# Retention stage of a hybrid decoder step: transposes over two sets of PSUM banks, query products after them, ScalarE spreads the sample queries; a sigmoid and squares move into a weight stream

## What is computed

```
q, k, v, g_ret = jnp.split(ret_cols.astype(f32), 4, axis=-1)
q = rotary(q...) * (RET_DK ** -0.5);  k = rotary(k...)
# retention_chunked, per chunk of tokens and head:
scores = jnp.einsum('bihd,bjhd->bhij', qc, kc) * dmat
o = jnp.einsum('bhij,bjhv->bihv', scores, vc)
o = o + jnp.einsum('bihd,bhdv->bihv', qc, s) * q_dec[None, :, :, None]
s = s * s_dec[None, :, None, None] + jnp.einsum('bjhd,jh,bjhv->bhdv', kc, k_dec, vc)
out_a = jax.nn.silu(g_ret) * head_norm(o, RET_GN_EPS)
...
gates = jax.nn.sigmoid(gate_cols.reshape(bsz, t, N_BRANCH, D_MODEL))
merged = jnp.sum(gates * jnp.einsum('btnc,ncd->btnd', branches, p['w_branch'][l]), axis=2)
...
m = rmsnorm(mem, p['mem_norm'][l])      # needs the squares of mem
```

## Time and profile before

| | us |
|---|---|
| median of 3 runs (lowest, highest) | 3109.57 (3106.17, 3111.55) |
| profiled execution, its own time | 3115.79 |
| span of its profile | 3114.1 |
| mean granted TensorE clock, share of full | 0.958 |

### The profile page before, as it was taken

How to read it: one execution, slowest core, us unless ns; L and a number is a source line. 1 busy time by engine, 2 the same in 40 slices (tenths; PEclk the granted TensorE clock), 3 DMA queues, 4 the chain that set the end, 5 groups by cost and what they waited for, 6 DMA issues and landing times. The chain is left out here.

```text
span 3114.1 us, 63966 instructions
## 1 busy us (share of the span) xinstructions
PE 2844.1 (91%) x25694; PEld 2645.1 (85%) x25694; DVE 1755.5 (56%) x2645; ACT 1253.0 (40%) x1739; POOL 521.4 (17%) x341
## 2 busy tenths in 40 slices
PE   7998989989988999899999988989898899998997
PEld 7998888777787898799889978987787788887997
DVE  4444764586576565544354458445756766655443
ACT  4534522254323443444254355222542234434542
POOL 0003650054400000000000046401543000000000
PEclk9999999999998999899999999999999989998998
DMA  4444340135374466344344443401454554663443
GB/s 164 148 148 140 118 141 18 37 115 181 109 278 162 158 211 220 129 149 148 116 152 148 149 134 112 126 24 34 138 176 144 224 213 128 221 222 119 149 148 105
DMA packets 119694, 448.21 MB, mean 144 GB/s; under 512 B 13648, under 2 KB 23920, under 8 KB 111664
## 3 DMA queue, kind: packets, MB, share of 16 engines
q1 hardware_dynamic: 97920, 329.78, 32.9%
q0 software_dynamic: 21552, 115.34, 10.1%
HBM read 397.04 MB, written 48.02 MB: 143 GB/s over the span
## 5 line engine op out<-in xcount | busy, mean ns | idle before, releaser
L1532 ACT ACTIVATE w_high<-ring 128x1024 fp32r<-128x1024 f32 x598 | 631.8, 1057 | 761.1 <-PE gemm_banks L902 320.9
L898 PE MATMUL gemm_banks<-in_high,w_high 128*128 128x320 f32 (+1 forms) x2720 | 802.3, 311 | 26.9 <-ACT w_high L1532 14.7
L1936 DVE TENSOR_TENSOR w_low<-ring,w_high 128x1024 fp32r<-128x1024 f32 x436 | 532.7, 1222 | 477.4 <-ACT w_high L1532 476.7
L899 PE MATMUL gemm_banks<-in_low,w_high 128*128 128x320 f32 (+1 forms) x2720 | 794.7, 308 | 0.0
L733 POOL TENSOR_TENSOR w_low<-ring,w_high 128x1024 fp32r<-128x1024 f32 x162 | 414.0, 2564 | 968.1 <-ACT w_high L1532 966.6
L898 PEld LDWEIGHTS gemm_banks<-in_high,w_high 128*128 128x128 f32 x2720 | 514.3, 189 | 33.8 <-issue 14.7
L899 PEld LDWEIGHTS gemm_banks<-in_low,w_high 128*128 128x128 f32 x2720 | 514.1, 189 | 1.7
L902 PE MATMUL gemm_banks<-in_high,w_low 128*128 128x320 f32 (+1 forms) x2720 | 451.0, 308 | 6.9 <-POOL w_low L733 3.9
L902 PEld LDWEIGHTS gemm_banks<-in_high,w_low 128*128 128x128 f32 x2720 | 408.8, 189 | 9.9 <-POOL w_low L733 5.1
L947 PE MATMUL gemm_banks<-in_high,w_high 128*128 128x320 f32 x640 | 209.2, 339 | 21.8 <-DVE arena L2062 16.7
L974 PE MATMUL gemm_banks<-act_high,w_high 128*128 128x320 f32 x704 | 208.3, 309 | 2.6 <-DVE arena L1985 2.6
(11 more groups left out here) (414 smaller groups left out, 4229.4 us busy)
## 6 DMA issues: line engine op xcount, KB each, us to landing
ring<-in_w SPq DMA_DIRECT2D x598, 512.0 KB, 3.6
arena<-in_kc POOLq DMA_DIRECT2D x14, 1024.0 KB, 6.6
arena<-in_vc POOLq DMA_DIRECT2D x14, 1024.0 KB, 7.3
out_fill<-stage SPq DMA_DIRECT2D x80, 160.0 KB, 4.0
arena<-in_ssm POOLq DMA_DIRECT2D x16, 512.0 KB, 13.6
out_s_ssm<-arena POOLq DMA_DIRECT2D x16, 512.0 KB, 14.0
arena<-in_ret POOLq DMA_DIRECT2D x16, 512.0 KB, 22.2
out_s_ret<-arena POOLq DMA_DIRECT2D x16, 512.0 KB, 7.1
```

The costliest lines, as they stand in the source:

```text
L898: mm(dst, w_high[:, slot, w(k)], in_high[:, k, 0:n], start=(k == 0), stop=False)
L899: mm(dst, w_high[:, slot, w(k)], in_low[:, k, 0:n], start=False, stop=False)
L1532: f(w_high[:, slot], ring[:, s, 0:D], ACT.Copy).then_inc(weights_high, 1)
L1936: tt(w_low[:, slot], ring[:, pos % RING, 0:D], w_high[:, slot].bitcast(F32), ALU.subtract).then_inc(weights_split, 1)
```

## The change

TensorE's three blocks of transposes go to banks 4 to 7, 0 to 3 and 4 to 7; the second waits for no copies, the third for those of the first. VectorE makes `qd` after the second block's copies, the eight sample products as one with a repeated table, and zeroes both mask buffers with two large memsets right after the third block. ScalarE writes the eight samples' queries into them, in eight copies after its own part of the transposes. In `ssd_out`'s stream, gate(2) now stands ahead of the split of chunk 4 and the squares of `mem` ahead of that of chunk 6.

```diff
--- before.py
+++ after.py
@@ -306,14 +306,13 @@
 def ret_steps(engine):
 
     if engine == "A":
-        return ["silu"] + [("tr", tb) for tb in range(3)]
-    out = ["qd"] if engine == "V" else []
-    out += [("tr", tb) for tb in range(3)]
+        return ["silu"] + [("tr", tb) for tb in range(3)] + ["qm"]
+    out = []
+    out += [("tr", 0), ("tr", 1), "qd", ("tr", 2), "qz"] if engine == "V" else [("tr", tb) for tb in range(3)]
     steps = [(tb, q) for tb in range(3) for q in range(2)]
     for m in range(6):
         out += [(*steps[m], "score")]
         out += [(*steps[m - 1], "out")] if 0 < m < 5 else []
-        out += ["qm"] if m == 2 and engine == "V" else []
     out += [("only", 0), ("only", 1)] if engine == "V" else []
     out += [("read", 0), ("read", 1), (2, 0, "out"), (2, 1, "out")]
     for j in range(4):
@@ -1319,14 +1318,14 @@
                 pe.wait_ge(psum_free, evacuated["ret"])
                 arrived(pe, layer, "vg_back")
                 for tb, (c0, n) in enumerate(TBS):
-                    if tb:
-                        need(V, ("tr", tb - 1))
-                        need(A, ("tr", tb - 1))
+                    if tb == 2:
+                        need(V, ("tr", 0))
+                        need(A, ("tr", 0))
                     for k in range(16):
-                        ins_ = tr(bank(4 + k // 4)[0:n, (k % 4) * P:(k % 4 + 1) * P], qkvg[:, 8 + k, c0:c0 + n], K("ident"))
+                        ins_ = tr(bank((4, 0, 4)[tb] + k // 4)[0:n, (k % 4) * P:(k % 4 + 1) * P], qkvg[:, 8 + k, c0:c0 + n], K("ident"))
                     hit(ins_, M, ("tr", tb))
-                need(A, ("tr", 2))
-                need(V, ("tr", 2))
+                need(A, ("tr", 1))
+                need(V, ("tr", 1))
                 steps = [(tb, q) for tb in range(3) for q in range(2)]
 
                 def score(m):
@@ -1381,7 +1380,7 @@
                     if 0 < m < 5:
                         out(m - 1)
                 arrived(pe, layer, "ret_states_here")
-                need(V, "qm")
+                need(A, "qm")
                 read(0)
                 read(1)
                 out(4)
@@ -1822,8 +1821,14 @@
                 A_.mark(f(qkvg[:, 24:32], qkvg[:, 24:32], ACT.Silu), A, "silu")
                 for tb, (c0, n) in enumerate(TBS):
                     need(M, ("tr", tb))
-                    A_(f(vtk[0:n, tb, 0:512], bank(6)[0:n, 0:512], ACT.Copy))
-                    A_.mark(f(vtk[0:n, tb, 512:1024], bank(7)[0:n, 0:512], ACT.Copy), A, ("tr", tb))
+                    A_(f(vtk[0:n, tb, 0:512], bank((6, 2, 6)[tb])[0:n, 0:512], ACT.Copy))
+                    A_.mark(f(vtk[0:n, tb, 512:1024], bank((7, 3, 7)[tb])[0:n, 0:512], ACT.Copy), A, ("tr", tb))
+                need(V, "qz")
+                for j in range(4):
+                    qm = (qm01, qm23)[j // 2][:, j % 2].rearrange("p a (b t) -> p a b t", t=SL)
+                    for b in (j, 4 + j):
+                        ins_ = f(qm[:, :, b], qd[:, :, P + b * SL:P + (b + 1) * SL], ACT.Copy)
+                A_.mark(ins_, A, "qm")
                 ret_headnorm(hsq, hroot, K("eps")[:, 1:2])
 
             def gate(j):
@@ -1875,10 +1880,13 @@
                 high_parts("ssd", rb_back)
                 arrived(act_, layer, "gates_back")
                 gate(1)
-                stream("ssd_out")
-                gate(2)
-                arrived(act_, layer, "mem_here")
-                A_.mark(f(msq, mem, ACT.Square), n_sq, "mem")
+                def between(i, c):
+                    if c == 2:
+                        gate(2)
+                    if c == 4:
+                        arrived(act_, layer, "mem_here")
+                        A_.mark(f(msq, mem, ACT.Square), n_sq, "mem")
+                stream("ssd_out", between)
                 high_parts("rwkv", rc)
                 stream("rwkv_out")
                 act_.wait_ge(psum_free, evacuated["rwkv_out"])
@@ -2394,18 +2402,19 @@
             def retention():
                 V, A, M = rt["V"], rt["A"], rt["P"]
                 arrived(dve, layer, "rettab_here")
-                V_(tt(qd[:, :, 0:P], qkvg[:, 0:8, P:TP], qtab, ALU.mult))
-                for b in SAMPLES:
-                    ins_ = tt(qd[:, :, P + b * SL:P + (b + 1) * SL], qkvg[:, 0:8, TP + b * SL:TP + (b + 1) * SL],
-                              qtab[:, :, 0:SL], ALU.mult)
-                    V_(ins_) if b < NS - 1 else V_.mark(ins_, V, "qd")
                 for tb, (c0, n) in enumerate(TBS):
+                    if tb == 2:
+                        V_(tt(qd[:, :, 0:P], qkvg[:, 0:8, P:TP], qtab, ALU.mult))
+                        qs, qo = (v.rearrange("p a (b t) -> p a b t", t=SL) for v in (qkvg[:, 0:8, TP:T], qd[:, :, P:P + C64]))
+                        V_.mark(tt(qo, qs, qtab[:, :, 0:SL].unsqueeze(2).to_broadcast([P, 8, NS, SL]), ALU.mult), V, "qd")
                     need(M, ("tr", tb))
                     kd = K("kdec" if tb < 2 else "s_kdec", 0, n)
                     for g in range(2):
                         ins_ = tt(split(ktok[:, tb], 8, P)[0:n, 4 * g:4 * g + 4],
-                                  bank(4 + g)[0:n, :].rearrange("p (a b) -> p a b", b=P), each(kd[:, 4 * g:4 * g + 4], P), ALU.mult)
+                                  bank((4, 0, 4)[tb] + g)[0:n, :].rearrange("p (a b) -> p a b", b=P), each(kd[:, 4 * g:4 * g + 4], P), ALU.mult)
                         V_(ins_) if g == 0 else V_.mark(ins_, V, ("tr", tb))
+                V_(nc.vector.memset(qm23, 0.0))
+                V_.mark(nc.vector.memset(qtab, 0.0), V, "qz")
                 steps = [(tb, q) for tb in range(3) for q in range(2)]
 
                 def score(m):
@@ -2435,20 +2444,10 @@
                         V_(tt(Sp[:, hs], Sp[:, hs], each(K("sdec")[:, hs], P), ALU.mult))
                         V_.mark(tt(Sp[:, hs], Sp[:, hs], st, ALU.add), V, (tb, q, "out"))
 
-                def masked_queries():
-                    for j in range(4):
-                        qm = (qm01, qm23)[j // 2][:, j % 2].rearrange("p a (b t) -> p a b t", t=SL)
-                        V_(nc.vector.memset(qm, 0.0))
-                        for h in range(2):
-                            b = 4 * h + j
-                            ins_ = copy(qm[:, :, b], qd[:, :, P + b * SL:P + (b + 1) * SL])
-                            V_(ins_) if b < NS - 1 else V_.mark(ins_, V, "qm")
                 for m in range(6):
                     score(m)
                     if 0 < m < 5:
                         out(m - 1)
-                    if m == 2:
-                        masked_queries()
 
                 def only(j):
```

## The result

| | median us (lowest, highest), runs |
|---|---|
| before, same chips | 3114.18 (3106.17, 3128.78), 12 |
| changed | 3097.7 (3090.14, 3103.32), 12 |
| ratio, 95% interval | 0.9939 (0.9924, 0.9953) |

By the ratio the kernel became 19 us faster (14.6 to 23.7; the two medians differ by 16.5); 22.6 were forecast. The forecast's 3086.6 and its range up to 3096 stood against a before of 3109.57, from which 19 less is 3090.6; the before of these runs is 4.6 higher. The profiled execution took 3102.74 us, 5.0 above its median, with a span of 3101.2. So the spans differ by less (12.9) than the medians, and I read stages, not the whole.

The account below looks back on a forecast made before the run. TensorE was taken as the bound (matmuls fill 91% of the span), so its idle and low-clock time decide. Retention's 11 plus the stream's 11.6 make 22.6, taken as 23 off 3109.6: 3086.6 us, range 3079 to 3096.

Parts of the forecast that it names:

- Second stretch: From ssd_out to rwkv_out: idle 5.31 to 0.92 and first chunk at full clock, 5.8 us less a layer, 11.6 in all.
- table load: Sign of being wrong: a table load appearing around the sigmoid moved into ssd_out's stream; none stood there before.
- VectorE's low parts: Rival ahead of rwkv_out: these end the wait, so the stream move fails; only 11 us from retention, about 3099, chance 0.04.
- The low clock only moves: Sign of being wrong: the low clock leaves the changed places only to turn up in denser ones; no size given.
- Retention: Start of retention: 5.0 + 2.3 + 2 x 2.6 = 12.5 us less, taken as 11 after the clock.
- the memsets: Ahead of the first score step on VectorE: two of 128x1024, 0.91 us each, new there and hidden by nothing.
- The first score step on VectorE: In retention: 5.0 us earlier in the second layer, 2.3 in the first; second layer 10.5 us after the first transposes.
- The fourth product's wait: In retention: with the masks off VectorE, TensorE's 2.60 us gap closes, 2.6 less in each layer.
- the masks on ScalarE had their cover: Eight ScalarE copies, at most 2.7 us, end ten microseconds ahead of read, so they cost nothing.
- I take off 0.8 a layer, between nothing and 1.5: Retention's charge for low clock behind a new 3.6 us TensorE wait ahead of the first product.
- The rule on transposes: The skill says transposes do not count as busy for the clock gate; the prediction said the trace disagrees here.
- the low clock: Rival: low clock from the transposes on costs 3 to 5 us a layer; total 14 to 18, 3092 to 3096, chance 0.12.

Follow-up runs that it names:

- the changed kernel once more: The changed kernel run again unaltered, for a second profile and as the mark for others; ratio 0.9939 of before.
- four filled into the wait: Changed kernel with four added matmuls in TensorE's wait ahead of the first product with v and one ahead of out; ratio 0.9912 of before.
- before with five filled in: The kernel before with five added matmuls of constants in TensorE's 5.3 us wait ahead of rwkv_out; ratio 1.0003.
- banks only: The kernel before with transposes over two sets of banks and qd behind the second block's copies, masks still on VectorE; ratio 0.9954.
- the 64.16 of the table: Ssd_out to out, second layer, of the changed kernel with qd behind the second score step and both memsets on GpSimd; ratio 0.9882 of before.
- the whole wait filled (ten): The kernel before with ten added matmuls of constants in TensorE's wait ahead of rwkv_out's first chunk; ratio 1.0015.

## Why the prediction was right, and what it mis-sized

**Second stretch: right.** Forecast 5.8 us a layer; ssd_out to out lost 5.8 and 6.2. The idle went to 0.92, the chunk to 5.33, the splits kept their pace with 0.24 us left behind the sigmoid, no table load appeared, and VectorE's low parts did not end the wait.

**What was missing there.** "The low clock only moves" was named as a way to be wrong, not put into the sum. Out to memk took 16.1 us in nine of the twelve layers of kernels whose stream is unchanged, and about 17 in eight of ten layers where it is changed and the wait ahead of `out` is not filled. On the mean of these layers some 0.6 us of the 5.8 are given back.

**Retention: right in sum, by terms that were off in both directions.** Forecast 12.5 less 1.6 for the clock, 11 in all; the stage lost 5.0 and 5.6 in the profile, 4.8 a layer over the six layers of three profiles. The sum was luckier than its layers: with 0.8 off for the clock it has 4.1 for the first and 6.8 for the second. The first lost more because its first block met the full clock this time (1.94 us for the 3.18 of before) and because before had lost 1.6 behind its 2.6 wait there; the second lost less because of the memsets' waits and the clock. And a low clock in the first block, which `qd` used to hide, now costs: 1.66 us in two of the six layers, which the sum has for the first layer only. The first score step on VectorE came 11.05 us behind the first transposes against 10.56 worked out for full clock; the half microsecond is the 0.28 us that each memset waits. The fourth product's wait closed, as said, and the masks on ScalarE had their cover. The term that failed in size is the clock: "I take off 0.8 a layer, between nothing and 1.5". From the first product to the update the changed kernel takes 21.7 to 22.4 us, and 20.05 with the wait filled, so it costs 1.6 to 2.3, above my upper end. Against before it costs less: in three of the eight layers with the old retention TensorE fell to the low clock behind the wait of 2.6 (24.3 us from the first product to the update, 22.7 in the others), 0.6 on the mean, which leaves about 1.2 a layer for the change. The wait was 4.26 us, not 3.6, for the memsets' waits again.

**The step that the prediction did not take** was to price the two halves against each other. It credited 2.6 us to the masks' move and charged 1.8 for the memsets. The runs say: on top of the two sets of banks the move costs 1.4 to 2.0 us a layer up to the update (32.1 against the 33.5 to 34.2 of the four layers whose first block ran at full clock), since it puts 2.4 us ahead of the first score step and the low clock behind the longer wait, for a gap of 2.6. By itself it gains 1.3. So up to the update the gain is the banks' and `qd`'s, and the masks' part takes 1.4 to 2.0 of the seven microseconds away again. Up to ssd_out the difference is 0.8 on the mean, inside the spread, and the whole times (0.9954 and 0.9963, with overlapping intervals) do not tell the two apart.

**The rule on transposes.** The trace after agrees with the one before, against the rule that the prediction cites from the Trainium skill (TensorE: Matmul & The Clock Gate, Part 4: PE-mode transpose), whose figures there are for bf16 where these are fp32: 48 transposes in a row, and a granted clock at full (1.91 us a block, in the profile above) with the scores behind them. In five layers of the new orders the first block met the low clock, and the clock rose with nothing but transposes run, here in the first layer of the changed kernel once more:

```profile
913.90:917.00 3.10, 3.10 (x16) 3.10 (x15) 0.69 (x1) 2.10 (x1) 0.00 (x0) 0.50 0.25 100
917.30:919.50 2.20, 2.20 (x22) 2.20 (x21) 1.59 (x3) 1.47 (x3) 0.00 (x0) 1.00 0.00 0
```

With four filled into the wait and the transposes as they are, no low clock came up to the update, in either layer. So in the changed kernel it came with the wait, not from the transposes. Transposes with waits between them are not settled by this: in the first layer of before with five filled in, the granted clock was 0.50 from 910.6 to 924.0, through all three blocks and their waits of 2.58 and 1.58; in the profile of before the same order rose after the first block.

**The sum.** 2 x 4.8 for retention and 2 x 6.0 for the stream, less 2 x 0.6 in `out`, make 20.4; measured 19 (14.6 to 23.7). These are lengths from single profiles, so that they meet the measured ratio so closely is partly luck. Of the rivals, the low clock came about in part, behind the new wait and not from the transposes on.

## What to carry to other kernels

When a wait is removed, look at the sum of what now stands ahead of the next one: in banks only TensorE ran at full clock behind waits of 1.9 and 2.6, and behind one of 4.3 it lost 1.6 to 2.3 us. A wait of 2.6 is not safe either: three of eight layers with the old retention met the low clock behind it. Work taken off a busy engine should go where nothing waits behind it; the same two memsets put 2.4 us ahead of the first score step, made TensorE wait 1.65 one step later, and cost it no wait on an engine that was idle. And move a long activation into a stream only after reading its idle between two splits: 2.45 us held 2.33.

## What the runs showed of the hardware, not expected

- With 4.4 us of TensorE's 5.3 us wait filled by matmuls and 1.02 left idle, the granted clock still fell (0.58 to 0.69 over the last 4.6 us of the chunk), in both layers. With an idle of 0.92 and no filling, rwkv_out's chunk kept the full clock in every layer of the changed stream, and ssd_out's in all but one (the 64.16 of the table). In before, with the whole wait filled (ten), it stayed at 1.00. So idle time just ahead does not decide it alone. What else does was not settled.
- GpSimd's memset of 128x1024 took 0.95 us against VectorE's 0.91, with VectorE's instructions beside it unchanged.
- The eight small ScalarE copies took 0.16 us each in a row, where the nearest row, a copy with a factor, had 0.336.
